# Building the one-hots of four tokens with one VectorE comparison, and multiplying the gates in on ScalarE

## The reference, cut to what matters

```python
s1, i1 = lax.top_k(sc[:, :, 0], 16)          # 8 heads, 128 sub-keys on each side
s2, i2 = lax.top_k(sc[:, :, 1], 16)
cand = (s1[..., :, None] + s2[..., None, :]).reshape(T, 8, 256)
best, ci = lax.top_k(cand, 16)
idx = e1 * 128 + e2                          # e1, e2: the two sub-key indices of a pick
g = jax.nn.softmax(best, axis=-1)
act = gelu(einsum('td,thkd->thk', xb, u_tab[idx]))
out = einsum('thk,thkd->td', g * act, v_tab[idx])
```

## Time and profile before

| | |
|---|---|
| median of three runs | 1793.0 us |
| the profiled execution | 1792.45 us |
| its span | 1790.6 us |
| TensorE busy | 1752.0 us, 98% |
| VectorE busy | 1416.7 us, 79% |
| ScalarE busy | 931.8 us, 52% |
| GpSimd busy | 422.5 us, 24% |

### The profile page before, as it was taken

The page is one execution under the profiler, slowest core; times in us unless marked ns, Lnnn a source line. Parts: engine busy times, 40 slices in busy tenths (PEclk is TensorE's granted clock), DMA queues, the critical chain, the costliest instruction groups (busy, mean ns, idle before and its releaser), DMA issues. The chain is left out here.

```text
span 1790.6 us, 28850 instructions
## 1 busy us (share of the span) xinstructions
PE 1752.0 (98%) x10950; PEld 1662.6 (93%) x10950; DVE 1416.7 (79%) x2144; ACT 931.8 (52%) x1399; POOL 422.5 (24%) x301
## 2 busy tenths in 40 slices
PE   9999999999999989999999999999999999999997
PEld 7887778788999989999999999999999989999997
DVE  4545785575589869999999998688888888888884
ACT  5454564444456545655555555555555545555553
POOL 0002300020132163111111112133333323343321
PEclk9999999999999989999999999999999999999998
DMA  7665445677577767777777779999999989999991
GB/s 245 206 188 158 148 142 174 179 252 238 170 219 217 218 210 242 258 239 229 229 229 231 231 234 324 301 355 352 352 345 349 345 297 359 349 362 391 355 350 61
DMA packets 126882, 462.59 MB, mean 258 GB/s; under 512 B 14720, under 2 KB 14816, under 8 KB 126096
## 3 DMA queue, kind: packets, MB, share of 16 engines
q1 hardware_dynamic: 95616, 347.65, 59.8%
q0 software_dynamic: 30992, 112.67, 17.2%
q10 hardware_dynamic: 144, 0.52, 0.1%
HBM read 455.73 MB, written 5.05 MB: 257 GB/s over the span
## 5 line engine op out<-in xcount | busy, mean ns | idle before, releaser
L1590 PE MATMUL PS<-W,HI 128*128 128x416 f32 x2048 | 438.4, 356 | 4.7 <-DVE OUTA L1233 2.6
L1550 PE MATMUL PS<-xT,HI 128*128 128x416 f32 x2048 | 440.1, 357 | 0.0
L671 ACT ACTIVATE HI<-V_RAW 128x1024 fp32r<-128x1024 f32 x256 | 271.8, 1062 | 292.5 <-PE PS L1590 168.5
L1590 PEld LDWEIGHTS PS<-W,HI 128*128 128x128 f32 x2048 | 368.3, 190 | 10.2 <-issue 2.8
L1550 PEld LDWEIGHTS PS<-xT,HI 128*128 128x128 f32 x2048 | 367.7, 190 | 3.8
L1123 DVE TENSOR_TENSOR V_LO<-V_RAW,HI 128x2048 fp32r<-128x2048 f32 x128 | 293.3, 2291 | 72.4 <-ACT HI L671 72.2
L671 ACT ACTIVATE HI<-RING_RAW 128x1024 fp32r<-128x1024 f32 x256 | 269.8, 1054 | 85.6 <-DMA RING_RAW<-u_t 83.0
L1556 PEld LDWEIGHTS PS<-xT,RING_LO 128*128 128x128 f32 x2048 | 269.0, 192 | 8.4 <-POOL RING_LO L442 7.3
L1556 PE MATMUL PS<-xT,RING_LO 128*128 128x208 f32 x2048 | 267.8, 274 | 7.1 <-POOL RING_LO L442 7.0
L1130 DVE TENSOR_TENSOR RING_LO<-RING_RAW,HI 128x1024 fp32r<-128x1024 f32 x225 | 266.4, 1217 | 7.1 <-ACT HI L671 7.1
L805 DVE TENSOR_TENSOR LO<-RAW,HI 128x1024 fp32r<-128x1024 f32 x132 | 163.1, 1237 | 136.3 <-PE PS L1323 98.5
(11 more groups left out here) (207 smaller groups left out, 1682.6 us busy)
## 6 DMA issues: line engine op xcount, KB each, us to landing
RING_RAW<-u_t SPq DMA_DIRECT2D x256, 512.0 KB, 4.6
V_RAW<-peer_v SPq DMA_DIRECT2D x256, 512.0 KB, 7.0
RAW<-w_in SPq DMA_DIRECT2D x80, 512.0 KB, 3.7
RAW<-w_out SPq DMA_DIRECT2D x32, 512.0 KB, 3.7
RAW<-wq_t SPq DMA_DIRECT2D x32, 512.0 KB, 4.7
x_spill<-X POOLq DMA_DIRECT2D x2, 1024.0 KB, 5.3
X1R<-x_spill POOLq DMA_DIRECT2D x8, 256.0 KB, 9.4
X<-x SPq DMA_DIRECT2D x3, 512.0 KB, 8.4
```

Of the source, the lines that this page charges most:

```text
L671: nc.scalar.activation(HI[:, n % HI_SLOTS, :], raw_of(n), ACT.Copy).then_inc(top_ready, 1)
L1550: return mm(PS[:, j % S_BANKS, 0:2 * ND].rearrange("p (a t) -> p a t", a=2), HI[:, n % HI_SLOTS, kk * P:(kk + 1) * P], xT[:, k, :, 0:ND], ...
L1590: return mm(PS[:, V_BANKS[i], 0:2 * ND].rearrange("p (a t) -> p a t", a=2), HI[:, v % HI_SLOTS, i * P:(i + 1) * P], weights_of(v), start=v ...
```

## The change

`one_hots` now makes both kinds of one-hots of a batch with one comparison of 1024 elements, into one new tile `ONE` (128 x 2 x 4 x 128). The gates are no longer multiplied in by VectorE: ScalarE does it in a new function `gates_into`, four copies of 128 elements with the gate as a per-partition scale, in place. It runs right after `put_gates` in ScalarE's list, and TensorE waits for it (semaphore `ones`); ScalarE waits for the comparison (a new semaphore `compared`). Steps 60 to 111 with a half operation become two of three instead of one of two, 34 instead of 26; counted from the code, scoring does 54 half operations instead of 46, and the value stage 138 instead of 146. The tile `PK4` moves to another place, and the matmul of `spread` reads its moving operand from one contiguous piece instead of four.

```diff
-HALF_STEPS = list(range(40, SPREAD0, 3)) + list(range(SPREAD0, SPREAD_END, 2)) + list(range(SPREAD_END, NKEYS - 3))
+HALF_STEPS = list(range(40, SPREAD0, 3)) + [j for j in range(SPREAD0, SPREAD_END) if j % 3] + list(range(SPREAD_END, NKEYS - 3))
...
-        PK4 = at("PK4", 108 * KB, [P, 3, NG], U32)
+        ONE = at("ONE", 108 * KB, [P, 2, TOKB, NKEYS])
...
+            def gates_into(b):
+
+                act.wait_ge(compared, b + 1)
+                for i in range(TOKB):
+                    t = b * TOKB + i
+                    ins = nc.scalar.activation(ONE[:, 1, i, :], ONE[:, 1, i, :], ACT.Copy, scale=EG[:, 2, t:t + 1])
+                ins.then_inc(ones, 1)
...
                 if 0 <= j - SPREAD0 < N_BATCH:
                     put_gates(j - SPREAD0)
+                if 0 <= j + 1 - SPREAD0 < N_BATCH:
+                    gates_into(j + 1 - SPREAD0)
...
                 dve.wait_ge(g_done, b)
-                v.tensor_tensor(ONE1[:], IOTA[:].unsqueeze(1).broadcast_to([P, TOKB, NKEYS]),
-                                EG[:, 0, b * TOKB:(b + 1) * TOKB].unsqueeze(2).broadcast_to([P, TOKB, NKEYS]), ALU.is_equal)
-                for i in range(TOKB):
-                    t = b * TOKB + i
-                    ins = v.tensor_scalar(ONE2[:, 4 * i:4 * i + 4, :], IOTA[:].rearrange("p (q c) -> p q c", q=4),
-                                          EG[:, 1, t:t + 1], EG[:, 2, t:t + 1], ALU.is_equal, ALU.mult)
-                ins.then_inc(ones, 1)
+                t0 = b * TOKB
+                v.tensor_tensor(ONE[:], IOTA[:].unsqueeze(1).unsqueeze(1).broadcast_to([P, 2, TOKB, NKEYS]),
+                                EG[:, 0:2, t0:t0 + TOKB].unsqueeze(3).broadcast_to([P, 2, TOKB, NKEYS]), ALU.is_equal)\
+                    .then_inc(compared, 1)
...
                 for t in range(TOKB):
-                    last = mm(PS[:, G_BANK + b % 2, t * NKEYS:(t + 1) * NKEYS].rearrange("p (q c) -> p q c", q=4),
-                              ONE1[:, t, :], ONE2[:, 4 * t:4 * t + 4, :],
+                    last = mm(PS[:, G_BANK + b % 2, t * NKEYS:(t + 1) * NKEYS], ONE[:, 0, t, :], ONE[:, 1, t, :],
                               start=True, stop=True)
```

More of the change, by code:

```diff
@@ L184, in hybrid_peer_block @@
         HOLES = at("HOLES", XT0, [P, 2 * KT, T])[:, :, ND:T]
-        ONE2 = HOLES[:, 16:32, 0:32]
         TMPL = HOLES[:, 16 - TMP_ROWS:16, 0:ND // TMP_ROWS]
@@ L219, in hybrid_peer_block @@
         EG = small("EG", [P, 3, ND])
-        ONE1 = small("ONE1", [P, TOKB, NKEYS])
+        off[0] = 200 * KB + 16 * ND + 4 * NS
+        PK4 = small("PK4", [P, 3, NG], U32)
         W1 = at("W1", XT0, [P, 2, 2, ND], FP32R)
@@ L280, in hybrid_peer_block @@
         copied = sem("copied")
-        ones, g_done, g_mul, g_put = sem("ones"), sem("g_done"), sem("g_mul"), sem("g_put")
+        compared, ones, g_done, g_mul, g_put = sem("compared"), sem("ones"), sem("g_done"), sem("g_mul"), sem("g_put")
         xs_saved, fgain_ready, xs_back = sem("xs_saved"), sem("fgain_ready"), sem("xs_back")
```

## The result

The changed kernel takes 1797.39 us (median of 11 runs) beside 1793.44 us for the kernel before in the same comparison: a ratio of 1.0026, 95% interval 1.0017 to 1.0034. It is slower by about 4 us: the interval leaves out "no change", while 0.2% (3.6 us) lies inside it. The forecast was 1795.9 us.

A forecast was written before the change was run, and what follows sets the result against it. TensorE was taken to bound the gate stage at 5.72 us a step. Lag of 4.9 us less cover of 1.96 gave plus 2.9 on 1792.45, 1795.35, and with 0.55 for the median 1795.9 us; range 1792.0 to 1801.0.

The forecast's parts named there:

- The bound: While gates are built, TensorE never waits, each step 5.72 us; time taken off VectorE is worth nothing.
- the loop: ScalarE and VectorE drive each other from one L704 to the next through comparison and scalings: 5.68 to 5.90 us.
- Two of the signs: Profile after: ScalarE's four scalings within 1.2 us; TensorE's idle time at `spread` ended by the scaling.
- the forecast: The loop passes TensorE's step late in the gate stage: plus 1 to plus 4.5 us, chance 0.40.
- the second rival: Same loop with s = 0.29, 5.72 to 5.94 us, never recovers: plus 5.4 us, 1798.4 us; chance 0.29.
- the price of one scaling: ScalarE's distance s from one 128-element scaling's start to the next: 0.28 us, four making 1.12 us a step.
- The lag: ScalarE falling behind TensorE's step: 4.0 us from the loop after about batch 8, 4.9 us with DMA waits.
- The 0.9 us from DMA waits: Lag from ScalarE's second `top` waiting for its transfer, at the point where the loop stops recovering: 0.9 us.
- The cover: Lag ScalarE may have before TensorE waits at its weight load for `spread`: 1.96 us.
- Nothing at the matmul of `spread`: TensorE's matmul now reading contiguous columns was taken at 0, between a 4 us gain and nothing.
- Half operations and value stage at 0: Eight more half operations put 10 us on VectorE in these steps, taken from the value stage; both costed at 0.
- the third rival: Less busy VectorE and fewer gathers clear the value stage's start, or contiguous matmul gains: about 4 us, 1789; chance 0.07.

The follow-up runs named there:

- the kernel with the loop cut: Changed kernel, but ScalarE does gates_into(b) one place later, right after the next low_half_out instead of right before it: 1794.45 us, ratio 0.9998.
- first profile: The profiled execution of the changed kernel, the slowest of its eleven runs: 1800.92 us, span 1798.9 us.
- the old half steps: Changed kernel with the half operations where they were before (46 in scoring, 26 of them in steps 60 to 111): 1799.76 us, ratio 1.0031.
- the second profile: The changed kernel run once more, unaltered: 1797.94 us, ratio 1.0024.
- five scalings: Changed kernel with a fifth copy a batch on ScalarE, same form and 128 elements, into unused memory: 1812.13 us, ratio 1.0104.

## Why the prediction was right, and where its sizes were off

**The bound.** Right: TensorE's step sets the stage, and time taken from VectorE gained nothing (the kernel with the loop cut is at 0.9998).

**The mechanism, its place and its sign.** Right: the loop, the stall at `spread`, late in the stage. Two of the signs named for it did not come: the four scalings last 1.28 us, not under 1.2, and the profile puts no idle time of TensorE down to them. The size, plus 4.0, fell between the forecast (plus 2.9) and the second rival (plus 5.4). It lies within the forecast's plus 1 to plus 4.5, but the lengths of the loop are the second rival's. The term that was sized wrong is the price of one scaling. I took s = 0.28 us, between a row with the operand in SBUF (0.29) and rows out of PSUM (0.256). Measured: 1.28 us for four with 0.39 for the last, (1.28 - 0.39)/3 = 0.297; single distances are 0.292 to 0.295 or 0.308 to 0.310. The SBUF row alone was the right guide. The estimate from the Trainium skill's figures ("ScalarE: Activation LUTs", section "What ACT_TABLE_LOAD costs"), 0.293 us, agrees with this trace too.

**The loop's length.** 5.68 to 5.90 forecast; 5.93 measured at batch 50. The rest of the terms held: 0.41 for 0.43, 0.29, 2.27, 0.52 for 0.53, 1.25 for 1.26; all of the difference is in the scalings, 1.19 for 1.12, less the 0.03 of the others. With 1.19 the second rival's 5.72 to 5.94 is what the trace shows.

**The lag.** The growth by 4.0 us was 4.5 (1.4 up to batch 30, then 3.1 in stalls), counted against the 5.74 us that TensorE took; against the 5.72 of the forecast it was 5.6, beside the second rival's 5.7. The 0.9 us from DMA waits was 0.62 at batch 1 in the first profile and 1.80 in the second, where the second rival had 1.7. Such a wait does stay, as that rival said: the old half steps and the second profile lost 1.0 and 0.8 us more by a single one. So the sum, with the prediction's terms in its own order, is 5.6 + 0.6 - 2.1 = 4.1 us of stage time in the first profile where 4.0 + 0.9 - 1.96 = 2.9 was forecast. That the forecast missed by no more is partly luck: once the gates had begun, no transfer of the first profile was late enough to lengthen a round.

**The cover.** 1.96 forecast, 2.06 measured. The stall was said to come in the last third; it came at batch 31 of 52 in one profile and 16 in the other.

**Nothing at the matmul of `spread`.** Right for `spread` itself (1.07 us in undisturbed steps, as before). The 0.02 us a step beside it were not foreseen, and their cause is not known. They are 1.0 of the stage's 4.1 us as it is split above, but by an estimate from the loop's lengths the whole would be about 4.1 without them too: with shorter steps TensorE would have met the loop earlier and waited more.

**VectorE.** Busy 22 us less in 772 to 1064, not 33. I had subtracted durations, which overlap. By starts, the old one-hots took 1.63 us of the engine and the new one 1.14; that is 0.49 a batch, not 0.83. Over 51 batches this is 25 us; seven more half operations in the window take 8 of them back, and one round fewer in it gives some 4.

**Half operations and value stage at 0.** Right for the half operations (0.9997 alone). Between the first and last high-part matmul of the value stage lie 629.8 us before and 631.5 in the first profile after, but 628.1 in the second of the same kernel: no change that can be told. TensorE still starts the value stage with a wait (1.56 us instead of 2.05), so the third rival's gain did not come.

## What to carry to other kernels

Moving work from a busy engine to an idle one gives nothing if a third engine sets the step, and it can cost if the moved piece stands between two engines' turns: add up one whole round across the engines that wait for each other, and compare it with the bound's step. Put such a piece behind the copy that the other engine waits for, not ahead of it; here that alone removed the stalls, 3.1 of the stage's 4.1 us. When a round is as long as the step, no delay is ever made up: what one late transfer costs stays to the end of the stage.

## What the runs showed of the hardware

A stall of 0.13 us in each step leaves TensorE's busy time at 292 of 292 us and names no waiter, since the profile models the ends of the matmuls; only the distance of the starts shows it. Of a delay of 0.40 us, with five scalings, it shows 0.25 as idle time and names who ended it. The granted clock stayed at 1.00, the full 2.4 GHz, through 21 such stalls. Four in-place scalings of 128 elements with a per-partition scale start 0.30 us apart on average and last 0.39 or 0.40 each.
